# The first microseconds of a three-block transformer kernel: the second column half of x behind the first weight unit, and matmuls on a tile of ones

## The reference, cut to what matters

```python
h = rms_norm(x, norm_mix_g[0])          # x * rsqrt(mean(x*x) + eps) * gain
proj = h @ ev_w_in[0]                   # 1024 x (512 q, 128 k, 128 v, 256 qi, 64 ki, 4 wi, 512 u)
q, k, v, qi, ki, wi, u = jnp.split(proj, offsets, axis=-1)
```

## Time and profile before

| | us |
|---|---|
| median of 3 runs (lowest, highest) | 957.46 (957.1, 957.81) |
| the profiled execution, its time | 958.34 |
| the profiled execution, its span | 956.2 |
| PE busy | 948.3 (99%) |
| DVE busy | 768.9 (80%) |
| ACT busy | 574.3 (60%) |

### The profile page before, as it was taken

The page is one execution under the profiler, slowest core; times in us unless marked ns, Lnnn a source line. Parts: engine busy times, 40 slices in busy tenths (PEclk is TensorE's granted clock), DMA queues, the critical chain, the costliest instruction groups (busy, mean ns, idle before and its releaser), DMA issues.

```text
span 956.2 us, 11751 instructions
## 1 busy us (share of the span) xinstructions
PE 948.3 (99%) x4599; PEld 782.8 (82%) x4599; DVE 768.9 (80%) x796; ACT 574.3 (60%) x610; POOL 76.1 (8%) x85
## 2 busy tenths in 40 slices
PE   8999999999999999999999999999999999999998
PEld 7878888888888888888888888888888888888887
DVE  4988999989865777999989885963565779998996
ACT  6656676566565756676666655566344456665672
POOL 3611101101000000101101021000000001101010
PEclk9999999999999999999999999999999999999999
DMA  8646888785464537879785365445435585987751
GB/s 300 262 133 201 250 297 230 199 285 132 159 216 134 170 96 219 240 258 251 195 293 147 131 210 196 147 162 191 156 124 205 160 267 147 314 234 211 252 132 45
DMA packets 125159, 190.07 MB, mean 199 GB/s; under 512 B 7208, under 2 KB 87216, under 8 KB 125104
## 3 DMA queue, kind: packets, MB, share of 16 engines
q1 hardware_dynamic: 110992, 172.73, 54.0%
q0 software_dynamic: 13952, 16.52, 9.9%
q10 hardware_dynamic: 160, 0.07, 0.0%
HBM read 188.24 MB, written 1.05 MB: 198 GB/s over the span
## 4 chain that ended last, share of the span: by engine, by line
PE 98%; ACT 0%; DMA 0%; SPq 0%; issue 0%; DVE 0%; ACTq 0%
PE psum L1916 28%; PE psum L1917 27%; PE psum L1921 27%; PE psum L2032 4%; PE psum L1909 2%; PE psum L1911 2%; PE psum L1910 2%; PE psum L2049 1%; PE psum L2397 1%; PE psum L2428 1%; PE psum L2073 0%; DMA raw<-in_ev_w_in 0%; ACT arena L855 0%; PE psum L2444 0%; PE psum L2055 0%; PE psum L2446 0%
## 5 line engine op out<-in xcount | busy, mean ns | idle before, releaser
L1277 DVE TENSOR_TENSOR low<-raw,high 128x2048 fp32r<-128x2048 f32 (+1 forms) x110 | 247.8, 2253 | 93.4 <-ACT high L783 93.4
L783 ACT ACTIVATE high<-raw 128x2048 fp32r<-128x2048 f32 (+1 forms) x113 | 213.4, 1890 | 90.8 <-PE psum L1921 84.0
L1916 PE MATMUL psum<-high,xh 128*128 128x512 f32 x664 | 264.0, 398 | 0.1
L1917 PE MATMUL psum<-high,xl 128*128 128x512 f32 x664 | 259.0, 390 | 0.0
L788 ACT ACTIVATE high<-arena 128x2048 fp32r<-128x2048 f32 x84 | 161.0, 1916 | 69.4 <-PE psum L1921 64.7
L1283 DVE TENSOR_TENSOR low<-arena,high 128x2048 fp32r<-128x2048 f32 x84 | 191.4, 2284 | 6.2 <-ACT high L788 6.2
L1921 PE MATMUL psum<-low,xh 128*128 128x512 f32 x664 | 172.9, 391 | 0.0
L1916 PEld LDWEIGHTS psum<-high,xh 128*128 128x128 f32 x664 | 124.7, 188 | 27.2 <-issue 1.2
L1921 PEld LDWEIGHTS psum<-low,xh 128*128 128x128 f32 x664 | 124.3, 188 | 26.1 <-issue 0.3
L1917 PEld LDWEIGHTS psum<-high,xl 128*128 128x128 f32 x664 | 124.8, 188 | 24.5
L1916 PE MATMUL psum<-high,mh 128*128 128x512 f32 x248 | 99.3, 400 | 0.0
(11 more groups left out here) (208 smaller groups left out, 1054.4 us busy)
## 6 DMA issues: line engine op xcount, KB each, us to landing
raw<-in_ffn_w SPq DMA_DIRECT2D x68, 512.0 KB, 6.7
arena<-in_ffn_w SPq DMA_DIRECT2D x64, 512.0 KB, 7.2
raw<-in_w_in SPq DMA_DIRECT2D x52, 512.0 KB, 4.6
raw<-in_od_w_qkv SPq DMA_DIRECT2D x24, 512.0 KB, 4.7
raw<-in_w_ffn_down SPq DMA_DIRECT2D x22, 512.0 KB, 6.1
arena<-in_ffn_w POOLq DMA_DIRECT2D x16, 512.0 KB, 7.6
arena<-in_w_ffn_gate SPq DMA_DIRECT2D x16, 512.0 KB, 6.4
arena<-in_w_ffn_up SPq DMA_DIRECT2D x16, 512.0 KB, 7.5
```

Source lines behind the costliest of these rows:

```text
L783: nc.scalar.activation(high[:, n % RING, 0:cols], raw[:, r, 0:cols], ACT.Copy).then_inc(high_ready, 1)
L1277: nc.vector.tensor_tensor(low[:, n % RING, 0:cols], raw[:, RING_AT[n] % RING, 0:cols], high[:, n % RING, 0:cols].bitcast(F32), ALU.subtrac ...
L1916: nc.tensor.matmul(out, sh, wh, start=start, stop=False, skip_group_check=True)
L1917: nc.tensor.matmul(out, sl, wh, start=False, stop=False, skip_group_check=True)
```

## The change

SP loads only the two tiles of column half 0 first, then units 0 and 1, then the two tiles of column half 1, then unit 2 and so on. PE transposes column half 1 no longer at the beginning, but inside `wide(U_KVQI, 0)`, between its high products of t = 0 and of t = 1. DVE's first instruction fills `selbias` with 1.0. PE's first work is 14 matmuls of 256 columns on that tile, before its wait for the identity; after the transposes of column half 0 come nine more. They write the unused columns 256 to 511 of bank 2, and nobody reads them. The orders of ACT and DVE are unchanged.

```diff
+BUSY_BANK, BUSY_FIRST, BUSY_MID = 2, 14, 9
...
-            for t, q in FIRST_ORDER:
+            def load_x(t, q):
                 sp.dma_start(xs[:, t, q * 512:(q + 1) * 512], x[0, t * P:(t + 1) * P, q * 512:(q + 1) * 512]
                              ).then_inc(x_in[t][q], 16)
...
             early = U_EOUT
+            for t, q in FIRST_ORDER[:2]:
+                load_x(t, q)
             for n in range(early):
                 load(n)
+                if n == FIRST_KVQI:
+                    for t, q in FIRST_ORDER[2:]:
+                        load_x(t, q)
...
+            nc.vector.memset(selbias[:].bitcast(F32), 1.0).then_inc(ones_ready, 1)
             dve.wait_ge(first_gain_T, 1)
...
+            def keep_busy(count):
+
+                for _ in range(count):
+                    nc.tensor.matmul(bank(BUSY_BANK, SEQ, 2 * SEQ), selbias[:, 0:P], selbias[:, 0:SEQ], start=True, stop=True, skip_group_check=True)
+
+            pe.wait_ge(ones_ready, 1)
+            keep_busy(BUSY_FIRST)
             pe.wait_ge(ident_in, 16)
             pe.wait_ge(first_gain_in, 16)
             nc.tensor.transpose(bank(FIRST_GAIN_BANK, 0, KD), gains[0:KD, 0:P], ident[0:KD, 0:KD]).then_inc(first_gain_T, 1)
-            for t, q in FIRST_ORDER:
+            for t, q in FIRST_ORDER[:2]:
                 first_x_T(t, q)
+            keep_busy(BUSY_MID)
+
+            def second_x_T():
+                for t, q in FIRST_ORDER[2:]:
+                    first_x_T(t, q)
...
             index_unit(0)
-            wide(U_KVQI, 0)
+            wide(U_KVQI, 0, mid=second_x_T)
             index_unit(1)
             wide(U_KVQI, 1, mid=index_kw)
```

More of the change, by code:

```diff
@@ L366, in program @@
         masks_ready = sem("masks_ready")
-        half_ready = sem("half_ready")
+        half_ready, ones_ready = sem("half_ready"), sem("ones_ready")
         q_gain_ready = sem("q_gain_ready")
```

## The result

The changed kernel is slower: 961.3 us median of 16 runs (957.77 to 967.92) against 957.55 for 16 runs of the kernel before (957.1 to 958.73), ratio 1.0036, 95% interval 1.0024 to 1.0048. I had predicted 956.8. The two kernels differ in spread as much as in the median: 10 of the 16 runs lie above 959.5, none of the kernel before.

What follows compares the result with a forecast made beforehand. PE's program plus its late start was taken as the bound. Start 0.38 and index unit 1.27 gained, transposes 0.87 lost, less about 0.1 for handovers: 0.7 us off 957.46, so 956.8; forecast 956.4 to 957.2, wider range 955.9 to 958.1.

Steps and rivals of the forecast that it cites:

- From there PE's work is the same in both kernels.: From the index transposes of line 2260 on, PE's work was taken as unchanged, so the sum was made there.
- a first wait of PE later than 20 us: Sign of a wrong forecast: the earlier PE would meet a transfer or DVE after 20 us.
- start 7.79 for 8.0: PE's start of the first index unit: predicted at 8.0 against 8.38 before, 0.38 us gained.
- transposes 0.79 for 0.87: Eight transposes of column half 1, moved inside the wide unit: 0.87 us lost, up to 1.70 at a low clock.
- The time of the rise: PE's clock rise, near 10.7 before, was put at about 7.4, within the nine filler matmuls.
- The 1.27 us for slow steps: First index unit's 12 matmuls, all at the high clock level: 1.40 us instead of 2.67, 1.27 saved.
- the median before already had an early rise: Rival: the usual execution before had a fast first index unit, so 0.5 us slower, 957.95; chance 0.12.
- ACT was in time for the index transposes: Rival at line 2260: ACT 0.6 us longer than thought, PE waits 0.45, 957.2; chance 0.14.
- the first transposes became fast only in part: Rival: the first transposes run at the high level too, PE starts at 7.45, gain 1.3, 956.1; chance 0.12.
- the ones did lift the clock: Rival: the ones do not lift the clock; 0.6 slower, 958.1, or 960.8 in the late form; chance 0.10.
- column half 1 landed in time: Rival: a column half 1 transfer lands 1.1 us later than its slot before, PE waits one for one; within 0.04.
- The case on the slower side that I worked out: Ones not lifting the clock: slow steps after PE's start at 8.28, 958.1, late form 960.8; chance 0.10.

Runs made afterwards that it cites:

- pool_waits_for_scores: Changed kernel with one added wait: GpSimd starts its subtraction of unit 7 only after DVE's four scores of the first query tile; 957.97 us, ratio 1.0003.
- after_quiet: Changed kernel with all three GpSimd operations (gain, pooling weights, subtraction of unit 7) held until the four scores are done; 957.99 us, ratio 1.0008.
- forced_meeting: Kernel before, with DVE waiting ahead of the third score for the event that also starts GpSimd's subtraction of unit 7; 965.06 us, ratio 1.0074.
- quarters: Changed kernel with GpSimd's subtraction of unit 7 as four instructions of 512 columns instead of one of 2048; 958.84 us, ratio 1.001.
- ones_only: Kernel before (its load order and transposes) with the 14 matmuls on ones ahead of the identity; 957.6 us, ratio 0.9997.
- ones_quiet: Kernel before with the 14 matmuls on ones and all three GpSimd operations held until the four scores are done; 957.66 us, ratio 1.0.

## Why the prediction was wrong

**The step that failed** is the premise under the sum: "From there PE's work is the same in both kernels." PE's is, but it has to wait in it: the sum put every wait of PE behind the index transposes at nothing, and there the runs showed 2.8 us in the profiled execution. I followed the new load order to the last tile of x and to unit 1, and stopped. The prediction's own list of signs had "a first wait of PE later than 20 us", but no price for it. With the new order unit 7, though issued at the same time (22.56 against 22.48), mostly lands before ACT asks for it, so GpSimd's 4.6 us subtraction starts among DVE's scores instead of behind them. Where they met, the last score took 4.66 us, and the 1.1 us of slack that DVE had before the pooling units was not enough. Removing the meeting from the changed kernel (pool_waits_for_scores) leaves 0.3 of the 3.75 us over the kernel before; making it in the kernel before, with an added wait of 1.6 us, adds 7.3. The trace of before had the warning in one row that I read over: the same three scores took 2.04 us, where after_quiet shows 1.13, because GpSimd's 1.36 us operation on the pooling weights ran beside them.

The Trainium skill has the rule: "SBUF — State Buffer", section "SBUF: two separate sides", says that VectorE and GpSimd share a pair of ports, and that a VectorE instruction with two SBUF inputs, or in one of its two-port modes, and a GpSimd instruction exclude each other for the whole instruction (with two inputs, only if the GpSimd instruction reads SBUF). The traces agree: the stall of 4.66 us against a GpSimd instruction of 4.62, the one in forced_meeting, the short one in quarters, the 2.04 against 1.13, and the 0.28 us of `MATCH_REPLACE8` beside the subtraction. The selection's `TENSOR_SCALAR` stood still too (1.07 us instead of 0.23); that it runs in a two-port mode is not shown by any trace.

**The sum itself** was nearly right up to 19 us (start 7.79 for 8.0, fast steps, transposes 0.79 for 0.87, no wait of PE for unit 1, for column half 1 or for ACT's `e_kw`; 0.68 us earlier in all for the 0.7). The time of the rise was not: it came during the first transposes (4.80 to 5.96), well ahead of my 7.4. The sum held all the same, since the index unit is all fast in both cases; that was luck. And the sum was set against the wrong ground. The 1.27 us for slow steps were real in the one trace that I read, but of four executions with the old beginning that have a trace, PE was at the index transposes at 18.89, 19.19, 19.26 and 19.59. Mine was the slowest, and the first had fast steps from 7.96 on and nothing left for the change to win. The times of the three of them without a forced meeting were 957.42, 957.99 and 958.34, against medians of 957.55 to 957.75, so the median execution should lie between the first two of them. This is argued from times; how often the kernel before rises early no run shows. The rival "the median before already had an early rise" had the mechanism of the fast one; its price, 0.5 slower, was too high for that execution, since the old beginning then also has a wait of 0.38 us for unit 1 that the new order removes. With the meeting gone the change is worth 0.3 us slower by the medians and nothing by the intervals.

**The rivals.** ACT was in time for the index transposes, the first transposes became fast only in part, the ones did lift the clock (all nine traces with ones ahead of the identity have the index unit in fast steps from its first matmul, against one of five without), column half 1 landed in time. The case on the slower side that I worked out was the wrong one: I looked for mishaps within the first 20 us.

**What stays open**: why unit 7 lands sooner with the new order, and which of the two moves in it, loads or transposes, does it; why the fast beginning of ones_only brought no shorter median; the rare long runs of the kernel before itself (4 of its 103 in the experiments' comparisons lie between 961.7 and 964.6), and of kernels that can't have the meeting of unit 7 (961.25, 961.95, 961.35); and SP's pause.

## What to carry to other kernels

A transfer that lands earlier starts everything behind it earlier, on other engines too: follow a reordered queue until the first unit whose wait for its transfer disappears, and ask what that wait had kept apart. The order of issues alone is not enough for this: unit 7 was issued no earlier and landed some 2 us sooner. The stall hides in an instruction's duration and not in any list of waits, so compare the mean duration of each form of instruction before and after. VectorE's two-input instructions (here its `TENSOR_SCALAR` too) and GpSimd's tensor instructions should be ordered by a semaphore and not by luck; where the order can't be given, short GpSimd instructions bound the stall. And a clock's rise seen in one profile is one draw: take a second profile before counting it as a cost that can be saved.

## What the runs showed of the hardware that was not expected

- One execution of the same beginning had fast steps from 7.96, others turned at 10.1 (two) and near 10.7, with the same work ahead of them. With 14 matmuls on ones from 1.3 us on, all nine traces have fast steps from the first index matmul, at 7.7 to 8.3.
- A wait of PE of 4.5 us was followed by some 4.6 us at half the clock, one of 2.8 us by none.
- GpSimd stands still for DVE as DVE does for GpSimd: its operation on 2 columns takes 0.23 us in ones_quiet, and took 2.34 in the trace before, where it started at 30.04 beside a DVE subtraction that ran from 30.02 to 32.30.
- DVE's `TENSOR_SCALAR` with one SBUF input waited for GpSimd's subtraction in four traces (0.53 to 1.07 us instead of 0.23); `MAX8` and `MATCH_REPLACE8` never did.
- An issue of SP at 83 to 87 us takes about 0.9 us longer when PE's program has 23 more matmuls near its start (2.81 to 3.01 against 2.02 us for four, in six traces against eight).
